# The key stream of a decoder step: its pieces over more weight units, the last four with their words in weight slots

## The reference, cut to what matters

```python
h = rms_norm(x, g_pre_mix)
q, k, v, a, gate = split(h @ w_in)            # 1024 -> 512, 512, 512, 512, 512
# 8 heads x 64; three dilated branches (window, dilation) = (128,1), (512,4), (2048,16)
# prompt: keys of the prompt; samples: cached keys and the new ones (concatenate([win_k, k]))
attn = combine_branches(...)                   # softmax over all branches together
u = a * sigmoid(gate)
c = causal_dwconv(u, conv_w) + conv_b          # width 31, 512 channels
c = silu(layer_norm(c))
x = x + rms_norm(concat(rms_norm(attn), rms_norm(c)) @ w_out)
x = x + rms_norm(cross_attention(x, mem_k, mem_v) @ w_xo)   # mem_k, mem_v from mem @ w_mk, w_mv
x = x + rms_norm((gelu(dwconv3(h @ w_up_act)) * (h @ w_up_lin)) @ w_down)
```

## Time and profile before

| | us |
|---|---|
| median of three runs | 1786.0 |
| the profiled execution | 1790.85 |
| its span | 1789.0 |
| TensorE busy (matmul), whole span | 1695.5 |
| VectorE busy, whole span | 1149.4 |
| GpSimd busy, whole span | 113.9 |

### The profile page before, as it was taken

The page is one execution under the profiler, slowest core; times in us unless marked ns, Lnnn a source line. Parts: engine busy times, 40 slices in busy tenths (PEclk is TensorE's granted clock), DMA queues, the critical chain, the costliest instruction groups (busy, mean ns, idle before and its releaser), DMA issues.

```text
span 1789.0 us, 29561 instructions
## 1 busy us (share of the span) xinstructions
PE 1695.5 (95%) x11614; PEld 1582.2 (88%) x11614; DVE 1149.4 (64%) x2050; ACT 859.5 (48%) x1616; POOL 113.9 (6%) x76
## 2 busy tenths in 40 slices
PE   7989858998999999999998999999999999999998
PEld 6988858875567999988778989999999999999998
DVE  5399998876775787434467567654576533676633
ACT  7312022374666766655456455443545533655433
POOL 0244443100000000000000000000000000000000
PEclk9999979999999999999999899999999999999999
DMA  9999999449423545544444334444445544444543
GB/s 316 255 242 225 210 221 237 119 157 340 166 84 106 163 148 165 165 123 125 144 128 118 95 107 132 139 131 141 134 138 153 148 133 141 132 139 145 149 134 102
DMA packets 417824, 284.02 MB, mean 159 GB/s; under 512 B 69675, under 2 KB 392353, under 8 KB 415887
## 3 DMA queue, kind: packets, MB, share of 16 engines
q1 hardware_dynamic: 412840, 273.31, 53.8%
q10 hardware_dynamic: 4847, 8.83, 1.5%
HBM read 226.97 MB, written 32.48 MB: 145 GB/s over the span
## 4 chain that ended last, share of the span: by engine, by line
PE 68%; SPq 10%; DMA 8%; DVE 8%; ACT 4%; issue 3%; DVEq 0%; ACTq 0%
PE bank L1311 64%; DMA PLANES<-HALVES 6%; PE bank L1308 4%; SPq L520 3%; SPq L511 2%; SPq L510 2%; DVE C L1901 1%; ACT whi L698 1%; SPq L465 1%; DVE wlo L1914 1%; DVE cv L1901 1%; DMA cached_t<-keys_turned 0%; DMA raw<-in_w_mk_dram 0%; DVE Pp L1905 0%; DVE Y L1901 0%
## 5 line engine op out<-in xcount | busy, mean ns | idle before, releaser
L1914 DVE TENSOR_TENSOR wlo<-raw,whi 128x1024 fp32r<-128x1024 f32 (+1 forms) x312 | 378.7, 1216 | 264.1 <-ACT whi L698 263.8
L1311 PE MATMUL bank<-op_hi,whi 128*128 128x352 f32 x1632 | 541.0, 331 | 4.9 <-DVE wlo L1914 2.8
L1311 PE MATMUL bank<-op_hi,wlo 128*128 128x352 f32 x1632 | 526.8, 323 | 0.0
L1311 PE MATMUL bank<-op_lo,whi 128*128 128x352 f32 x1632 | 525.8, 322 | 0.0
L698 ACT ACTIVATE whi<-raw 128x1024 fp32r<-128x1024 f32 (+1 forms) x312 | 325.3, 1043 | 407.5 <-DMA raw<-in_w_in_dram 149.7
L1311 PEld LDWEIGHTS bank<-op_hi,whi 128*128 128x128 f32 x1632 | 308.5, 189 | 14.7 <-issue 10.0
L1311 PEld LDWEIGHTS bank<-op_lo,whi 128*128 128x128 f32 x1632 | 309.8, 190 | 0.6
L1311 PEld LDWEIGHTS bank<-op_hi,wlo 128*128 128x128 f32 x1632 | 308.1, 189 | 0.0
L1901 DVE SCALAR_TENSOR_TENSOR C<-U,cw,C 128x1024 f32<-128x1024 f32 x120 | 185.9, 1549 | 3.7
L1311 PE MATMUL bank<-h1hi,whi 128*128 128x352 f32 x480 | 161.5, 336 | 15.8 <-DVE wlo L1914 15.8
L1311 PE MATMUL bank<-fhi,whi 128*128 128x352 f32 x528 | 171.1, 324 | 0.0
(11 more groups left out here) (284 smaller groups left out, 2234.3 us busy)
## 6 DMA issues: line engine op xcount, KB each, us to landing
raw<-in_w_up_dram SPq DMA_DIRECT2D x132, 512.0 KB, 3.8
raw<-in_w_down_dram SPq DMA_DIRECT2D x48, 512.0 KB, 4.0
PLANES<-HALVES SPq DMA_DIRECT2D x128, 112.0 KB, 3.5
keys_turned<-WORDS SPq DMA_DIRECT2D x32, 448.0 KB, 3.8
cached_t<-keys_turned SPq DMA_DIRECT2D x8, 1792.0 KB, 9.9
raw<-in_w_out_dram SPq DMA_DIRECT2D x24, 512.0 KB, 4.1
raw<-in_w_xq_dram SPq DMA_DIRECT2D x24, 512.0 KB, 4.1
raw<-in_w_xo_dram SPq DMA_DIRECT2D x24, 512.0 KB, 4.1
```

Source lines behind the costliest of these rows:

```text
L1311: return pe.matmul(out, lhsT, rhs, start=first, stop=last, skip_group_check=shared)
L1914: dve.tensor_tensor(wlo[v % SLOTS][:, 0:nk, :], raw[v % SLOTS][:, 0:nk, :], whi[v % SLOTS][:, 0:nk, :].bitcast(F32), ALU.subtract).then_in ...
```

## The change

Four edits.

1. `PIECES_AT`: one step of the key stream after units 8, 9, 10, 12 to 16, 18, 19, 20, 22, 23 (13 steps instead of 16 by unit 23) and one after each of units 24 to 35 (before: 16 after units 24 to 33, and two after 34). So 24 steps stand ahead of the load of unit 35, where 34 stood.
2. The rest of the stream follows unit 35: steps 25 to 29; then the wait that pieces 26 and 27 are kept, and the tables; step 30; then the wait for unit 35 and `window(0)`; and behind it steps 31, 32 and 33.
3. The last four pieces (28 to 31) have their words in two new places, `WORDS2` and `WORDS3`, in slots 0 and 1 of the weight ring, so the tables need not wait for them. GpSimd waits for units 32 and 33 before it writes there, and the three loads of `w_out` units 36 to 38, which take slots 0 to 2, come behind all three windows and wait for the last words to be kept (before, they followed the tables).
4. The second and the third place of `cached_t` change their roles: `window(1)` now goes where the convolution's input was and waits for the layer norm's last square; `window(2)` goes over `HALVES` and `PLANES` and waits for the last join.

```diff
-    PLACES = (47104, 160064, 119808)
+    PLACES = (47104, 119808, 160064)
...
+    WORDS += [place("WORDS2", RING, [P, KEYS]), place("WORDS3", RING + 5504, [P, KEYS])]
...
-    PIECES_AT = {u: 1 for u in range(NT, 3 * NT)}
-    PIECES_AT.update({3 * NT + i: n for i, n in enumerate((2, 1, 2, 2, 1, 2, 1, 2, 2, 1))})
+    LATE = PIECES - 4
+    PIECES_AT = {u: 1 for u in (*range(NT, 3 * NT, 2), 9, 13, 15, 19, 23, *range(3 * NT, XFIRST))}
+
+    def words_of(p):
+        return WORDS[p % 2 + (2 if p >= LATE else 0)]
...
-        for u in range(SLOTS, XFIRST + SLOTS - 1):
+        for u in range(SLOTS, XFIRST):
...
-            if u == XFIRST - 2:
-                for p in range(p, PIECES + 2):
-                    key_stream(p)
-            if u == XFIRST - 1:
-                for i in range(2):
-                    sp.wait_ge(*at(f"kept{i}", PIECES - 2 + i))
-                load(wt[:, :], A["prompt_bias"], "tables", "p")
-                load(ws[:, :], A["sample_bias"], "tables", "s")
...
+        while p < LATE + 2:
+            key_stream(p)
+            p += 1
+        for i in range(2):
+            sp.wait_ge(*at(f"kept{i}", LATE - 2 + i))
+        load(wt[:, :], A["prompt_bias"], "tables", "p")
+        load(ws[:, :], A["sample_bias"], "tables", "s")
+        key_stream(LATE + 2)
         sp.wait_ge(*at("unit", LAST_IN))
         window(0)
-        window(1)
+        for p in range(LATE + 3, PIECES + 2):
+            key_stream(p)
         sp.wait_ge(*at("csq_used", 2 * CH - 1))
         sp.wait_ge(*at("cn", (CONV_ORDER[CH - 1], CT - 1)))
+        window(1)
+        sp.wait_ge(*at("joined", (PIECES - 1, 1)))
         window(2)
+        for u in range(XFIRST, XFIRST + SLOTS - 1):
+            for i in range(2):
+                sp.wait_ge(*at(f"kept{i}", PIECES - 2 + i))
+            weight(u)
...
+            if p in (LATE, LATE + 1):
+                pool.wait_ge(*at("unit", LAST_IN - 3 + p % 2))
+            words = words_of(p)[:, :].bitcast(U16).rearrange("p (n h) -> p h n", h=2)
```

More of the change, by code:

```diff
@@ L525, in keep_keys @@
             sp.wait_ge(*at("joined", (p, 1)))
-            sp.dma_start(A["keys_turned"][b, :, k, :], WORDS[p % 2][:, :]).then_inc(*mark(f"kept{p % 2}", p, 16))
+            sp.dma_start(A["keys_turned"][b, :, k, :], words_of(p)[:, :]).then_inc(*mark(f"kept{p % 2}", p, 16))
         def key_stream(p):
@@ L676, in join_keys @@
                 pool.wait_ge(*at(f"kept{p % 2}", p - 2))
-            words = WORDS[p % 2][:, :].bitcast(U16).rearrange("p (n h) -> p h n", h=2)
+            if p in (LATE, LATE + 1):
+                pool.wait_ge(*at("unit", LAST_IN - 3 + p % 2))
+            words = words_of(p)[:, :].bitcast(U16).rearrange("p (n h) -> p h n", h=2)
             for h in range(2):
```

## The result

The changed kernel takes 1795.8 us (median of 6 runs, 1795.1 to 1799.6), beside 1784.4 for the kernel before on the same chip: a ratio of 1.0063, 95% interval 1.0046 to 1.0080. It is slower, by 8 to 14 us; the forecast was 1784.5 with a range of 1772 to 1794. (The 1786.0 of the table before is the median of the first three runs of the kernel before; 1784.4 is that of six.) In the changed kernel the lines of VectorE, TensorE and GpSimd stand 13 higher (L1901 is L1914 now), those of SyncE 4 to 11 higher (L465 is L469, L579 is L590).

What follows compares the result with a forecast made beforehand. VectorE's taps and `wlo` were taken to bound the input stage. The terms -24.1 (E), +3 (layer norm), +16.6 (M), +3.2 (L) sum to -1.3 us: 1786.0 becomes 1784.7, stated as 1784.5, range 1772 to 1794.

Steps and rivals of the forecast that it cites:

- the faster one: Rival: the input stage gives more than the attention's start costs; middle 1777 us, chance 0.33.
- L: Landing and first use of sample 3's keys in the attention; forecast 415.3 against 416.6 before.
- the late stream: Rival: key-stream step 30 isn't done at U, each us delays M; 1788 at 9 us a step, chance 0.07.
- U: End of unit 35's last product, behind the layer norm; forecast 364.8, 21.1 us earlier than before.
- The spread does nothing to E: Rival: VectorE is bound by its taps, other waits replace those two; +8.6 us, 1793, chance 0.07.
- E: End of VectorE's taps in the input stage; forecast 323.1 against 347.2 before, a gain of 24.1 us.
- The late joins hold up the layer norm: Rival: joins 26 to 29 cost 2.34 us each, lower clock 2 us more; +7 us, 1793, chance 0.13.
- First tap: Start of VectorE's taps: earlier, as one stream step less precedes unit 13's weights; 95.14 to 88.4, 6.7 us gained.
- The waits of 1.94 and 7.99: VectorE's waits at 201.72 and 315.56 for late weights in the input stage; they go, 9.9 us gained.
- (c): Six GpSimd joins fewer beside VectorE's taps before E, at 1.25 us each; 7.5 us gained, bounds 0 to 14.
- Layer norm: Stretch from E to U: 38.7 us as before, plus 3 us for four joins now falling into it.
- M: First masked maximum of the attention, behind join 31 and the memsets; forecast U + 20.9, before U + 4.3, 16.6 us lost.

Runs made afterwards that it cites:

- e7: Kernel before with GpSimd's joins of pieces 2 to 31 cut to 8 of 896 columns; ratio 0.9989 to the kernel before.
- e6: Changed kernel with GpSimd's joins of pieces 2 to 27 cut to 8 of 896 columns; ratio 0.9926 to the kernel before.
- e1: Changed kernel with GpSimd's memsets of QW and QO moved ahead of the joins of pieces 30 and 31; ratio 1.0059 to the kernel before.
- e2: Changed kernel with the three w_out loads moved from behind window(2) to behind window(3), sample 3's keys; ratio 1.0061 to the kernel before.
- e3: Changed kernel with the edits of both e1 and e2; ratio 1.0026 to the kernel before.
- e4: Changed kernel with the key stream's last steps issued ahead of the wait for unit 35 and window(0); ratio 0.9989 to the kernel before.
- e11: Kernel before with only the stream's spread; last ten steps, tables and w_out loads behind unit 35's load; ratio 0.9963 to the kernel before.
- e8: Kernel before with only the three w_out loads moved behind window(2); ratio 1.0038 to the kernel before.
- e5: Changed kernel with the edits of both e4 and e2; ratio 0.9952 to the kernel before.
- e9: e4 with window(3), sample 3's keys, issued ahead of V's outputs; ratio 0.9953 to the kernel before.

## Why the prediction was wrong, point by point

- **The rivals**: the faster one is excluded (L came later, not earlier), and so is the late stream: step 30 was issued by 354.5, 14 us ahead of U. *The spread does nothing to E* is excluded by E itself. (That rival's +8.6 on 1786.0 gives 1794.6, not 1793; the measured 1795.8 lies above either.) *The late joins hold up the layer norm* comes below.
- **First tap**: 88.4 forecast, 88.15 measured. Right.
- **The waits of 1.94 and 7.99 vanish**: right, no wait of over 0.5 us is left. From the first tap to E 252.1 us became 239.4; 9.9 of these 12.7 are the waits. But they aren't a gain apart from the joins': in e7 the time that the joins give back turns into more of such waits.
- **Joins, step (c)**: the step that failed. The prediction read that the taps and `wlo` set the pace, since VectorE was busy for 240.5 of 259 us, took the mean price of a join there, 1.25 us, and gave six joins fewer a gain of 7.5 us. e7 shows that all 29 joins cost the old kernel 1.5 us at E, since the queue set the pace. What the spread did was to free the queue; VectorE with its joins became the bound, at 1.51 us a join and not 1.25 ((1514 - 1285) x 120 and (1559 - 1230) x 22, 34.7 us in all, by 23). So (c) was worth 36.1 - 34.7 = 1.4 us in VectorE's busy time, not 7.5. The old mean was low partly because two of the 29 joins, those at 87.34 and 310.55, fell into VectorE's waits for weights, took their undisturbed 2.33 us and slowed nothing (36.1 by 27 is 1.34); in the changed kernel no join finds such a wait. E: 327.6 instead of 323.1, 4.5 us. The two joins in the kernel before:

```profile
87.34 2.33 POOL L679 COPY WORDS<-PLANES 128x896 uint16<-128x896 uint16 x2 [5.32 <-DMA PLANES<-HALVES]
310.55 2.33 POOL L679 COPY WORDS<-PLANES 128x896 uint16<-128x896 uint16 x2 [4.00 <-DMA PLANES<-HALVES]
```

  From the exclusive lock of the Trainium skill ("SBUF — State Buffer", "Who interferes with whom") the prediction worked out that a join costs its whole 2.34 us; by the changed kernel's rows it costs 1.51 us of VectorE's time, and by e6 1.13 us of E (26.1 for 23), so the full price isn't borne out. That one side stands while the other works is borne out by the rows of one join, two taps and two copies of the changed kernel:

```profile
107.61 2.24 DVE L1914 SCALAR_TENSOR_TENSOR C<-U,cw,C 128x1024 f32<-128x1024 f32 x1
109.88 2.05 DVE L1914 SCALAR_TENSOR_TENSOR C<-U,cw,C 128x1024 f32<-128x1024 f32 x1
107.61 1.22 POOL L692 COPY WORDS<-PLANES 128x896 uint16<-128x896 uint16 x1 [4.70 <-DMA PLANES<-HALVES]
108.74 2.17 POOL L692 COPY WORDS<-PLANES 128x896 uint16<-128x896 uint16 x1
```

  The first copy takes nearly its undisturbed time and the tap that starts with it 0.95 us over its 1.29; the second copy starts under that tap and takes 1.0 us over its 1.18, and the tap behind takes 0.77 over. So they hold each other up by turns, and a copy costs a tap less than its own length.
- **Layer norm**: U - E forecast 41.7, measured 41.0 in this execution. The number was met partly by luck. The code is the same up to U in e1, e2 and e3, and there it took 46.4, 45.0 and 42.2. And the 3 us were added for the joins, but the rows show another price as well, which the prediction had only in a rival: behind its wait of 14.48 us for the taps' sums TensorE's granted clock was 0.50, the level of 1.2 GHz, from 328 to 334, where it was 1.00 before (wait of 0.96). In e6, where TensorE doesn't wait there, it is 1.00 and U - E 38.6, with one full join and four cut ones in the stretch. Joins and clock aren't parted further: with 11 and 12 copies in the stretch, against 8 in the changed kernel, U - E is 41.3 in e4 and 47.7 in e11. So the rival of the late joins was nearer than its chance of 0.13.
- **M**: forecast U + 20.9, measured U + 23.3. Its order was as described: transposes landed at U + 9.8 (9.4 forecast), but the parting landed at U + 17.1 and not U + 14.6, as the partings of 30 and 31 stand behind one another.
- **What hangs on M**: wrong in part. The sum made L follow M. In e1 M was 19 us nearer to U and L only 4.9. What L hangs on is SyncE's queue: window(1) waits in the changed kernel for the layer norm's last square, which is behind M, and had it not, it would still stand behind piece 31's keep (e1: at U + 20.0 instead of U + 24.5).
- **L - M**: forecast 29.6, measured 32.8: the term for `w_out` was mis-sized. It took 2.3 us "by the issues", and the three loads stood for 10.25. e8 has the same place alone: 11.01 us on the queue and 5.4 to 5.9 of L - U.

The four misses at L, 4.5 - 0.7 + 2.4 + 3.2, make 9.4 us: 424.7 instead of 415.3. By these profiles L is 8.1 behind before, and the medians differ by 11.3; the other 3.2 us are in no stretch that the profiles show. The profiled execution of before took 1790.9 at a median of 1784.4, and both profiles of that kernel fell above its median; which stretch its fastest runs save on stays open.

In short, the loss has two places on one queue. The spread gives 19.7 us at E and 17.4 at U. The steps of pieces 30 and 31 behind U take 15.9 of L - U (e4), and the `w_out` loads 5.4 to 7.0 (e8, e2, e5). The two make 21 to 23 of the 25.5 us by which L - U rose; the rest (e5 has 33.3 against 30.7) stays open. e11, which has the spread and neither of the two, keeps the old distance (31.5) and is 4 to 9 us faster than before.

## What to carry to other kernels

An engine that is busy for 93% needn't be the bound if its busy time is stretched by contention: look at whether the queue that feeds it ever waits for a free slot. If it doesn't, as here from 88 to 327, the queue or its transfers come first, and 37 us less of the engine's busy time bring 1.5 us. A mean price of contention, taken where the engine has waits, is too low for where it has none (1.25 and 1.51 us a join). When work is moved behind a point, follow the loads on the issuing queue up to the first one that TensorE waits for, and price each transfer between by its issue in that crowd, not by its issue in an empty one, less what the issues behind it then take less (e8: 11.01 us of issue cost 5.4 to 5.9); the first instruction that comes late may cost nothing (e1). Once one load is early enough, the next on the same queue is the wait (e9), so the gain of a reordering is counted at the last of them.

## What the hardware showed that was not expected

- A weight's load is issued mostly in 0.37 to 0.57 us in the input stage, three of them in 10.25, 11.01 and 13.10 us behind windows of 1792 KB each that are still moving, and in 4.00 us in e11, with only the tables ahead of them. V's eight outputs take 3.87 us to issue in e9 and 7.93 in e5.
- A GpSimd copy beside VectorE's taps: 1957 ns on average, 1178 alone; 23 joins put 34.7 us on VectorE. Beside copies of 8 columns, a tap's mean is 1284 ns, its old median.
- The same layer norm took 41.0 and 46.4 us in two kernels that don't differ up to there; over its last 14 us the mean granted clock was 1.00 in the one (TensorE's wait ahead of it was 0.70 us) and 0.76, a mean over the levels of 2.4 and 1.2 GHz, in the other (2.94 us).
